# Projections in the order k q v q k v, and the edge passes of both attentions inside the neighbouring projections

## The reference, cut to what matters

```python
mod = silu(c) @ ada_w + ada_b                   # six vectors of 2048
sh1, sc1, g1, sh2, sc2, g2 = split(mod, 6)
h, hc = modulate(rms_norm(x)), modulate(rms_norm(ctx))
proj = h @ w_in                                 # qa ka va | qb kb vb | gates
a = neighbourhood_attention(qa, ka, va, ...)    # 8 heads of 128, one softmax over
                                                # a window with bias and 256 context keys
s = einsum('bqhmd,bkhmd->bhmqk', rope(qb), rope(kb)) * 64 ** -0.5   # two maps m per head
p = softmax(s); p = p[:, :, 0] - lam * p[:, :, 1]
b = rms_norm(p @ vb, g) * (1 - lambda_init)     # 8 heads of 128
y = sigmoid(ga) * (a @ w_pa) + sigmoid(gb) * (b @ w_pb)
x = x + g1 * (y @ w_out)
x = x + g2 * conv_ffn(modulate(rms_norm(x), sh2, sc2)); return rms_norm(x)
```

## Time and profile before

| | |
|---|---|
| median of 3 runs (lowest to highest) | 1766.71 us (1766.47 to 1768.63) |
| profiled execution, its span | 1768.22 us, 1766.5 us |
| TensorE busy, mean granted clock | 1705.2 us (97%), 0.993 of full |
| DVE busy, ACT busy, POOL busy | 1091.8, 752.6, 105.3 us |
| HBM read | 366 MB, mean of all DMA 209 GB/s |

### The profile page before, as it was taken

One profiled execution on the slowest core, in us unless ns is written; L12 is line 12 of the kernel. 1 busy time (PEld: TensorE's weight loads), 2 busy tenths in 40 slices (PEclk: granted clock), 3 DMA queues, 4 the chain that ended last, 5 costly groups with the idle time before them and its releaser, 6 DMA issues.

```text
span 1766.5 us, 23906 instructions
## 1 busy us (share of the span) xinstructions
PE 1705.2 (97%) x8863; PEld 1399.9 (79%) x8863; DVE 1091.8 (62%) x1375; ACT 752.6 (43%) x949; POOL 105.3 (6%) x155
## 2 busy tenths in 40 slices
PE   4999999999999989999999999999999999999996
PEld 1468888877888668888888888888888888888885
DVE  1338768867774785545545676666666666655556
ACT  2232223612223465444444465555555555444443
POOL 0003221222220000000000000000000000000000
PEclk9999999999999999999999999999999999999998
DMA  9999888279874306665656646666666666555551
GB/s 351 387 382 331 280 284 289 75 251 317 277 260 120 110 1 236 189 194 189 188 193 213 191 135 183 188 189 188 189 190 189 189 190 190 198 194 190 193 195 64
DMA packets 160716, 369.31 MB, mean 209 GB/s; under 512 B 11471, under 2 KB 12127, under 8 KB 159758
## 3 DMA queue, kind: packets, MB, share of 16 engines
q1 hardware_dynamic: 139808, 291.98, 51.0%
q0 software_dynamic: 19728, 72.04, 12.4%
q10 hardware_dynamic: 1118, 4.44, 0.6%
HBM read 366.26 MB, written 2.16 MB: 209 GB/s over the span
## 4 chain that ended last, share of the span: by engine, by line
PE 88%; DMA 5%; DVE 4%; issue 1%; ACT 1%; SPq 0%; DVEq 0%; POOLq 0%; POOL 0%; ACTq 0%
PE ps L1624 20%; PE ps L1623 10%; PE ps L1633 10%; PE ps L1634 10%; PE ps L1635 10%; PE ps L1937 4%; PE ps L1935 4%; PE ps L1936 4%; DMA raw<-in_ada_w 4%; PE ps L1548 3%; PE ps L1549 2%; PE ps L1550 2%; DMA ada_raw<-in_ada_w 2%; PE ps L1620 1%; PE ps L1540 1%
## 5 line engine op out<-in xcount | busy, mean ns | idle before, releaser
L964 DVE TENSOR_TENSOR w_lo<-raw,w_hi 128x1024 fp32r<-128x1024 f32 x480 | 584.6, 1223 | 465.3 <-ACT w_hi L593 464.3
L593 ACT CAST w_hi<-raw 128x1024 fp32r<-128x1024 f32 x480 | 503.4, 1049 | 857.0 <-PE ps L1635 335.5
L1624 PE MATMUL ps<-h2T,w_hi 128*128 128x512 f32 x1320 | 462.5, 394 | 0.0
L1623 PE MATMUL ps<-h2T,w_lo 128*128 128x256 f32 x1320 | 366.5, 278 | 0.0
L1624 PEld LDWEIGHTS ps<-h2T,w_hi 128*128 128x128 f32 x1320 | 247.5, 188 | 53.6
L1623 PEld LDWEIGHTS ps<-h2T,w_lo 128*128 128x128 f32 x1320 | 247.9, 188 | 4.0
L1633 PE MATMUL ps<-w_hi,hT 128*128 128x512 f32 x512 | 200.7, 392 | 0.0
L1635 PE MATMUL ps<-w_hi,hT 128*128 128x512 f32 x512 | 199.4, 389 | 0.0
L1634 PE MATMUL ps<-w_lo,hT 128*128 128x512 f32 x512 | 199.2, 389 | 0.0
L1036 DVE SCALAR_TENSOR_TENSOR ada_acc<-ada_raw,silu_c,ada_acc 128x512 f32<-128x512 f32 x240 | 180.0, 750 | 29.5 <-DMA ada_raw<-in_ada_w 11.3
L1935 PE MATMUL ps<-w_hi,f_hi 128*128 128x512 f32 x352 | 137.0, 389 | 1.0 <-DVE conv_in L1375 1.0
(11 more groups left out here) (213 smaller groups left out, 1964.4 us busy)
## 6 DMA issues: line engine op xcount, KB each, us to landing
raw<-in_ffn_w_up SPq DMA_DIRECT2D x176, 512.0 KB, 3.8
raw<-in_w_in SPq DMA_DIRECT2D x152, 512.0 KB, 4.6
ada_raw<-in_ada_w POOLq DMA_DIRECT2D x128, 512.0 KB, 6.0
raw<-in_ffn_w_down SPq DMA_DIRECT2D x88, 512.0 KB, 3.5
raw<-in_ada_w SPq DMA_DIRECT2D x64, 512.0 KB, 10.6
raw<-in_w_out SPq DMA_DIRECT2D x32, 512.0 KB, 3.7
raw<-in_w_branch_a SPq DMA_DIRECT2D x16, 512.0 KB, 3.7
raw<-in_w_branch_b SPq DMA_DIRECT2D x16, 512.0 KB, 3.7
```

The source lines that it names most:

```text
L593: act.copy(w_hi[:, s % SPLIT_SLOTS, :], raw[:, s, :]).then_inc(hi_ready[s], 1)
L964: dve.tensor_tensor(w_lo[:, s % SPLIT_SLOTS, :], raw[:, s, :], w_hi[:, s % SPLIT_SLOTS, :], ALU.subtract).then_inc(lo_ready[s], 1)
L1623: pe.matmul(ps[:, b + t, 0:SEQ], w_lo[:, row4(s), at], high(kc), start=False, stop=False)
L1624: mm = pe.matmul(o, w_hi[:, row4(s), at], both(kc), start=False, stop=(kc == KC - 1))
```

## The change

- The projections go k q v q k v in both branches. The modulation groups are spread over jobs 1 to 11 anew; in job 5 their steps fall in the first six slots, in job 11 in the first four.
- Passes 0 and 1 of each attention run inside the last projection before it (a v job): scores after slot 5, the turns and values after tiles of slots 6 and 7, scores 2 and 3 after the last tiles. Passes 14 and 15 end inside the first job after it (6 and 12): values 14 and turn 15 after the first tile, values 15 after tile 2 (in job 12 after the first tile of slot 1).
- The v results of jobs 5 and 11 are read tile by tile, all by ACT. All eight rotations run in jobs 8, 10 and 11.
- The scale of the differential scores is folded into q on reading, so that the scaling of the maximum goes. The difference of the maps is taken with one weight (map 0 unscaled plus map 1 times -lambda sum0 / sum1), and the head's result is multiplied by 1 / sum0 on reading, by ACT for even passes and by DVE for odd ones.
- The spreads of g1 and g2 are transposes of broadcast columns, 16 each; g2's is read in quarters. In the last out job, slots 4 to 7 run tile 0 first and then tile 1; the second norm goes by token tile. The split of the neighbourhood result (aT) moves from job 11 to behind that of bT. The k loads of the head wait for `lo_ready` of two slots earlier.

```diff
-PROJECTIONS = [("k", KA), ("k", KA + GROUP), ("v", VA), ("v", VA + GROUP), ("q", QA), ("q", QA + GROUP),
-               ("k", KB), ("k", KB + GROUP), ("v", VB), ("v", VB + GROUP), ("q", QB), ("q", QB + GROUP)]
+PROJECTIONS = [("k", KA), ("q", QA), ("v", VA), ("q", QA + GROUP), ("k", KA + GROUP), ("v", VA + GROUP),
+               ("k", KB), ("q", QB), ("v", VB), ("q", QB + GROUP), ("k", KB + GROUP), ("v", VB + GROUP)]
-ADA_JOBS = [1, 1, 2, 2, 3, 3, 4, 5, 6, 6, 7, 7, 8, 8, 9, 9]
+ADA_JOBS = [1, 2, 2, 3, 4, 4, 5, 5, 6, 6, 7, 8, 9, 10, 10, 11]
+ADA_SPAN = {JOB_DIFF - 1: 6, JOB_MERGE - 1: 4}
...
+                    if s >= 2:
+                        sp.wait_ge(lo_ready[s - 2], 1)
...
+            def read_values(j, t, done):                      # ACT
+                act.wait_ge(used[7], j + 1)
+                g = (PROJECTIONS[j - JOB_NA][1] // GROUP) % 2
+                act.copy(v_sb[:, t, g * GROUP:(g + 1) * GROUP], ps[:, 4 + t, :]).then_inc(done, 1)
...
+            na_exponent(0)                                    # ACT behind job 5
+            round_hi(JOB_DIFF, 0)
+            na_exponent(1)
+            na_read_turned(0)
+            round_hi(JOB_DIFF, 1)
+            na_read_turned(1)
+            scale_ctx(2)
+            na_exponent(2)
+            scale_ctx(3)
+            round_hi(JOB_DIFF, 2)
+            for t in (2, 3, 0, 1):
+                read_values(last, t, kv_read)
...
+            def df_difference(n):                             # DVE
+                weight = row_sum[:, n % 3, 1:2]
...
+                dve.reciprocal(row_inv[:, n % 3, :], row_sum[:, n % 3, :]).then_inc(df_recip, 1)
+                dve.wait_ge(df_recip, n + 1)
+                dve.tensor_scalar(weight, row_inv[:, n % 3, 1:2], lam[:, 0:1], row_sum[:, n % 3, 0:1], ALU.mult,
+                                  ALU.mult).then_inc(df_lam, 1)
+                dve.wait_ge(df_lam, n + 1)
+                dve.scalar_tensor_tensor(diff_e[:, n % 2, 0, :], diff_e[:, n % 2, 1, :], weight,
+                                         diff_e[:, n % 2, 0, :], ALU.mult, ALU.add).then_inc(df_probs, 1)
...
+            def first_na(s, t):                               # TensorE, in job 5 (first_df in job 11 alike)
+                if (s, t) == (5, 3):
+                    pe.wait_ge(*results_read(JOB_DIFF - 2))
+                    sum_mod(ada_groups(JOB_DIFF - 1)[0], JOB_DIFF)
+                    na_scores(0)
+                    na_scores(1)
+                if (s, t) == (6, 3):
+                    na_turn(0)
+                if (s, t) == (7, 0):
+                    na_turn(1)
+                if (s, t) == (7, 1):
+                    na_values(0)
+                if (s, t) == (7, 2):
+                    na_values(1)
+                    na_scores(2)
+                if (s, t) == (7, 3):
+                    na_scores(3)
+            def last_na(s, t):                                # TensorE, in job 6
+                if (s, t) == (0, 0):
+                    na_values(N - 2)
+                    na_turn(N - 1)
+                if (s, t) == (0, 2):
+                    na_values(N - 1)
...
-                        spread(g1_spread, 0, 4)
+                        for kc in range(KC):
+                            mm = pe.transpose(ps[:, 4 + kc // 4, (kc % 4) * P:(kc % 4 + 1) * P],
+                                              mod[:, kc:kc + 1].to_broadcast([P, P]), ident)
...
+            for s in range(SPLIT_SLOTS, SLOTS):               # last out job
+                take(JOB_OUT + 3, s)
+                mm = out_unit(3, s, 0)
+            mm.then_inc(out_tile, 1)
+            for s in range(SPLIT_SLOTS, SLOTS):
+                out_unit(3, s, 1).then_inc(used[s], 1)
```

More of the change, by code:

```diff
@@ L862, in modulate2 @@
                                    scale=gain2[:, kc:kc + 1]).then_inc(modulated2_ready, 1)
-            for m in range(4):
-                modulate2(m)
+            modulate2(0)
+            modulate2(1)
+            for s in (2, 3):
+                round_hi(JOB_UP, s)
+                modulate2(s)
             for s in range(SPLIT_SLOTS):
@@ L1201, in _ @@
                         read_mod(j)
+                    if j == last and s == SLOTS - 1:
+                        read_mod(JOB_MERGE)
+                        df_maxima(0)
+                        df_maxima(1)
                     if j > JOB_DIFF or s >= SPLIT_SLOTS - 1:
@@ L1243, in _ @@
+                    if j == last and s in (4, 5):
+                        rope(s + 2)
+            df_difference(0)
+            split_lo(JOB_MERGE, 0)
+            df_difference(1)
+            split_lo(JOB_MERGE, 1)
+            df_maxima(2)
+            df_result(1)
+            df_maxima(3)
+            split_lo(JOB_MERGE, 2)
+            for n in range(EARLY, N):
+                df_difference(n)
                 if n + 2 < N:
                     df_maxima(n + 2)
-                if n in LATE_ROTATIONS:
-                    rope(LATE_ROTATIONS[n])
@@ L1314, in add_out @@
                 at = slice(g * GROUP, (g + 1) * GROUP)
-                for t in range(TOK):
+                for t in tiles:
                     if g == 3 and t == 0:
@@ L1673, in projection @@
                 for s in range(SLOTS):
-                    if s == SLOTS - 1 and j in (JOB_DIFF - 1, JOB_MERGE - 1):
-                        pe.wait_ge(*results_read(j - 1))
-                        for n in range(2):
-                            (na_scores if j < JOB_DIFF else df_scores)(n)
                     take(j, s)
@@ L1786, in _ @@
                     df_values(n - 1)
                 df_turn(n)
-            df_values(N - 1)
             def part(t):
                 return lambda kc, n: t[:, kc, n * P:(n + 1) * P]
-            def spread(n, col, b):
-                for kc in range(KC):
-                    mm = pe.matmul(ps[:, b + kc // 4, (kc % 4) * P:(kc % 4 + 1) * P],
-                                   mod[:, col + kc:col + kc + 1].to_broadcast([P, P]), ident,
-                                   start=True, stop=True)
-                mm.then_inc(n, 1)
@@ L1861, in _ @@
                     pe.wait_ge(yT_ready, 4)
-                for s in range(SLOTS):
+                for s in range(SPLIT_SLOTS if g == 3 else SLOTS):
                     if g == 0 and s == 6:
```

542 lines of the change are left out of this document (330 added, 212 removed).

## The result

The changed kernel takes 1768.28 us (median of 12 runs, 1766.43 to 1773.46), the kernel before 1766.01 (median of 12, 1762.25 to 1768.63 and one of 9674.07, which no trace explains). The ratio on record, 1.0021 with an interval of 1.0012 to 1.0031, is not the quotient of these medians: they differ by 2.3 us, the ratio says 3.7, slower by 2 to 5 us. In the runs beside the experiments the kernel before had medians of 1763.9 to 1764.1. Forecast was 1770.1, +3.4. The two profiled executions say something else at first sight: 1767.22 with a span of 1765.5 after, 1768.22 and 1766.5 before. That is -1.0 us. Both kernels spread over 6 us and more from run to run, so the profiles are read for places and durations, the timed runs for the sum.

What follows compares the result with a forecast made beforehand. TensorE, busy 97% of the span, was taken to bound the kernel. Terms summed to +1.2 us, plus 2.2 for a likely clock drop: +3.4, 1770.1 us against the timed median; range 1758 to 1778, the forecast's own 1766 to 1774.

Steps and rivals of the forecast that it cites:

- job 2, wait and clock: TensorE at job 2 waits 3.6 us for `mod`, then loses 2.9 at half clock: +6.3 with rounding (bounds 0 and 9).
- jobs 4 and 10: After a shorter q job, TensorE waits for `mod` without a clock drop: +2.0 us each, +4.0 (bounds 0 and 9.8).
- job 6 less job 7: Job 6 waits for slot 3's split, with half clock, +8.6 us; job 7's wait and half clock go: net +2.4.
- job 12: The late differential result puts squares, reduce and small step before slot 3's split: +2.4 us (bounds 0 and 5.3).
- neighbourhood attention: TensorE's work there stays the same; lost time falls from 7.3 to 4.7 us: -2.6 (bounds -5 and +0.3).
- differential attention: The pass cadence falls from DVE's 2.90 us to TensorE's 2.64: -7.8 us (bounds -9 and -2).
- out to up: From the out job's end to the up job, 7.8 us instead of 9.5: -1.7 (bounds -4 and +1.5).
- new drops of the clock: Four new gaps of 2.4 to 2.6 us; at least one likelier than not drops the clock: +2.2 us taken.
- Slack at jobs 2 and 6: Rival: DVE or the loads are earlier there than counted, gaps stay under the drop: 1757.5 us, one alone 1762; chance 0.28.
- The cadence at 2.80: Rival: attention loops do not speed up, 2.6 of the 7.8 us not won: 1770.5 or 1772.7; chance 0.10.
- Several drops: Rival: all new gaps drop the clock, 4 x 2.9 on +1.2 is +12.8, 1779.5 us; chance of several drops 0.13.
- Transposes as idle: Rival: transposes from out to up count as idle, 2.9 us of half clock follow, 1770.8 us; chance 0.04.

Runs made afterwards that it cites:

- Three experiments: Each against the changed kernel: mod read one slot earlier (ratio to before 0.9968); two pairs of group 8 loaded early (1.0001); slot 3 of job 12 split first (1.0015).
- the two scalings: Changed kernel with the map difference as before (first map multiplied by its inverse sum, results read without scaling): 1774.20 us, ratio to before 1.0055.
- the filled gap: Changed kernel with 20 identity transposes in the second norm's gap (1768.26 us, ratio to before 1.0025), or 10 products there (1768.20 us, 1.0026).
- one number in each of two lines: Changed kernel with read_mod one slot earlier in DVE's list, in all jobs but 6: 1757.28 us, ratio to before 0.9968.

## Why the prediction was right, point by point

| term | forecast | from the two profiles |
|---|---|---|
| job 2, wait and clock | +6.3 | +6.6 (4.96 gap, 1.6 clock) |
| jobs 4 and 10 | +4.0 | +2.6 (gaps 1.75 and 1.31, less one matmul each) |
| job 6 less job 7 | +2.4 | -0.3 (4.3 + 1.7, less 3.3 + 3.0) |
| job 12 | +2.4 | +2.6 |
| neighbourhood attention | -2.6 | -1.8 (what remains up to job 7's start, which moved by +12.0) |
| differential attention | -7.8 | -7.9 (what remains from there to the g1 spread, 689.30 to 690.79) |
| g1 spread | -1.8 | -1.8 (3.73 to 1.91) |
| out to up | -1.7 | -1.7, and +1.1 of clock behind the up job's start |
| new drops of the clock | +2.2 | counted in the rows above |
| sum | +3.4 | -0.7 (rows unrounded), with -0.2 at the start -1.0 |

Two rows are remainders, so that the sum agrees with the profiles is no check of it.

- **The mechanisms** held at every place: each wait that was forecast came, at its place, and no other of size. `mod` of job 2 at 165.2 for 164.5; job 6's first step at +12.7 for 13.1 and its split at +23.2 for 24.2; out to up 7.8 for 7.8; the pass in the differential loop 2.58 for 2.64. Three experiments took the waits at jobs 2, 4 and 10, at job 6 and at job 12 away, but for 0.2 to 0.6 us each.
- **Mis-sized:** the wait at job 6, 4.1 for 5.7 (the split 1.0 us earlier, TensorE some 0.6 later than counted), and jobs 4 and 10, 2.6 for 4.0 (0.4 and 0.8 us less each). And the price of a drop: I took 2.9 us for those at jobs 2 and 6 from the earlier trace rows, and they cost 1.6 and 1.7. The 1.4 of the first window of the earlier trace rows was as near.
- **Luck in the terms that hit.** Job 2's +6.3 had a wait 1.4 us too short and a drop 1.3 too dear. The differential attention gained some 1.0 us more by its cadence (16 x 0.06), and lost 1.7 to a drop behind the turn of pass 2, which this term did not hold.
- **A reading that was wrong.** The prediction says that the new gaps lie between an idle stretch that kept the clock and one of 3.1 us that lost it. Its 3.10 at job 7 is idle time, but its 3.2 at the first differential turn is from start to start; the idle time there is 2.6. And it left out the gap ahead of the first window of the earlier trace rows, at 0.50, with 2.4 us idle:

```profile
PE ps L1727 <- DVE scores L1172: 2.4, 1, 2.4
```

So the trace of before already had drops behind 2.4 and 2.6 us of idle time, as long as the new gaps, and more than the one drop that was added to the sum (2.2 us) was to be reckoned with. Two came in the profile.

- **The clock's share of the sum.** The two profiles differ by -1.0 us, the timed runs by +2.3 in their medians and +3.7 in the ratio (2.1 to 5.5). The profiled execution of the changed kernel is 1.1 us under its median, that of the kernel before 2.2 over its own, which is all of the 3.3 from -1.0 to +2.3. The clock is a likely cause, but not a shown one: the changed kernel's drops cost 6.6 us in its profile, but 7.4 to 10.7, 9.1 in the mean, in the seven other kernels with the one weight that keep two gaps of 3.9 us or more. No second profile of before was taken: this stays open. The forecast, 4.4 us above what the two profiles show, met the timed difference with stalls that were too high in the sum, by 1.4 at jobs 4 and 10 and 2.7 at jobs 6 and 7; that it came within 1 us of the ratio is in part luck.
- **The rivals.** Slack at jobs 2 and 6: not seen. The cadence at 2.80: not seen with the change, and it is what the two scalings give. Several drops: four of them came in the profile, two of which I had in the sum as certain (jobs 2 and 6). Transposes as idle: not borne out at this place by the filled gap, where the granted clock was 1.00; by the Trainium skill ("TensorE: Matmul & The Clock Gate", Part 4, PE-mode transpose) it should have fallen, and it did not.

## What to carry to other kernels

A job that is made shorter takes its cover away from whatever another engine does beside it: read from its list where the result that the next job needs stands, and move that read to where its input is ready. Here one number in each of two lines was worth 9 us and the sign of the change. Where an engine's work is late as such, moving an item of it ahead only moves the wait; start its loads earlier instead. Moving passes into neighbouring jobs pays their fill and drain again at the place where they now meet the queues of the other engines, so look at what stands ahead of the first pass behind the seam.

## What the runs showed of the hardware

- Gaps, start to start on TensorE, in the profiles of the changed kernel and the experiments: all 20 of 3.9 us or more (at jobs 2, 6 and 7) were followed by the 1.2 GHz level, as were all ten of 3.04 in the differential attention. Of those of 2.82 in the neighbourhood attention 6 in 11 were, of those of 2.73 to 2.79 at job 12 4 in 10, of those of 2.81 in the norm 10 in 11. One of 2.50 at job 4 was. In the kernel before those of 2.79, 3.19 and 3.49 were, one of 2.58 was not. One of 1.90 was, with one of 1.43 right behind it; one of 1.91 without such a second one was not, nor any other of 1.3 to 2.1. So between 2.5 and 2.9 us it differs from one execution to the next, at the same gap of the same code.
- A drop cost 1.6 to 1.7 us in most cases and 2.3 to 3.0 in the rest, which is as far as the windows reach. It begins up to 1.1 us behind the gap.
- A clock of 0.50 from 18.5 to 42.4 us, where TensorE was busy for two thirds of the time and the DMA share was 1.04, moved nothing: its 116 instructions kept TensorE busy for 15.88 us, 15.75 at full clock in the kernel before. Job 2 starts at 155.4 us there and at 155.0 and 155.1 in the two other kernels with such a stretch, at 155.1 to 155.8 in the ten without.
- The profile's releaser of a wait for several semaphores can be the wrong engine: "ACT v_sb" for a turn that DVE's last write released, shown by moving DVE's split alone.
